# RWKV stage: the k projection first, the elementwise chain written between the weight splits of r and v

## The chip, the cores and the metric

The kernel runs on one core of a Trainium2 chip. The metric is the device time of one execution in microseconds, as the median of several runs. The core has a matrix engine (TensorE, PE in the rows), a vector engine (VectorE, DVE), an activation engine (ScalarE, ACT), GpSimd (POOL), and SyncE (SP), which here issues all the transfers. Each engine works through its own instructions in written order and waits for others on semaphores.

## The reference, cut to what matters

The whole computation is a chain of transformer stages on 256 tokens of width 1024 (`T` = 256, `D` = 1024, `C` = 8 chunks of 128 features). The change touches one of them, the RWKV7 time mixing of the second layer:

```python
xx = jnp.pad(h, ((0, 0), (1, 0), (0, 0)))[:, :-1] - h
xr, xw, xk, xv, xa, xg = [h + xx * mu[i] for i in range(6)]
r = xr @ w_r
w = -jax.nn.softplus(-(w0 + jnp.tanh(xw @ w1) @ w2)) - 0.5
k = xk @ w_k
v = xv @ w_v
a = jax.nn.sigmoid(a0 + (xa @ a1) @ a2)
g = jax.nn.sigmoid(xg @ g1) @ g2
kk = heads(k * k_k)
kk = kk / jnp.maximum(jnp.sqrt(jnp.sum(kk * kk, -1, keepdims=True)), 1e-12)
k = k * (1 + (a - 1) * k_a)
decay = jnp.exp(-jnp.exp(heads(w)))
def step(state, inp):
    sa = jnp.einsum('bhij,bhj->bhi', state, -kk_t)
    state = (state * d_t[:, :, None, :] + sa[..., None] * (kk_t * a_t)[:, :, None, :]
             + v_t[..., None] * k_t[:, :, None, :])
    return state, jnp.einsum('bhij,bhj->bhi', state, r_t)
bonus = jnp.sum(r_ * k_ * r_k.astype(f32), -1, keepdims=True) * v_
```

`exp(-exp(w))` is `exp(-KAPPA * sigmoid(...))` with `KAPPA` = exp(-0.5), so that running sums of the sigmoid (`gs`) give the decays. The recurrence is done in chunks of 64 tokens. For that, the chain computes `A = -kk * (decay up to the token before)`, `B = kk * a * growth`, `K = k * growth` and `R = r * decay`, where `decay` is exp(-KAPPA gs) and `growth` is exp(KAPPA gs).

A second task is woven in: `mod = cs @ ada_w[i] + ada_b[i]` for two later layers ("modulation"), with 48 weight slots of 1 MB.

## The kernel before, in words

Weights come through a ring of six slots of 1 MB (`Weights`, `RING`); SyncE issues the loads in one order written out in advance, each after the signals that free its slot. A product in fp32 is made of three products of split operands (`mm3`, lines 714 to 716): every slot holds two *units* of 128 output columns, ScalarE writes the high part of a unit's weights (`split_act`, line 672), VectorE the remainder (`split_dve`, line 678), and TensorE then does 24 products (`columns_pe`). The sources are split likewise (lines 696 and 704). `depth` is the number of buffers for split units, 2 in this stage.

The stage runs as follows. The norm; the shifted difference `xx`; six mixings `h + xx * mu` (line 1976), of which two buffers `m0` and `m1` hold two at a time; four low-rank hidden products (line 2002) and sixteen output products (line 2011) that give `sg` and `a`; then 24 units in the order r, k, v. Behind unit 23 stands the elementwise chain: scans, the sum of squares per head by TensorE (`heads_pe`, line 1989), Ln and Exp for its inverse root, then kk, A, the k factor, k, the bonus sums, K and R on VectorE and ScalarE, and `sum_before`, `b` and `B` on GpSimd (lines 2189 to 2194).

Between the steps of this chain `Modulation.fill` puts pieces: a piece is the column sum of the one before (line 1882), eight products with a weight slot (line 1893) and a copy by ScalarE (line 1901). 5, 5 and 2 pieces are written into the chain; the others come one per step of the inverses in the blocks (11 steps) and two ahead of each of a block's two chunks.

Four *blocks* (`block_pe` and its companions) do the recurrence, one for 512 features and 128 tokens each; a block begins with twelve transposes (line 2232). Behind them are the normalisation, the gate and the output product.

Of the kernel before, what the change touches and what calls it, by code (L numbers as in the profile page):

```python
# [110 lines left out]
def lay_out(a):  # L111
# [19 lines left out]
    for layer in range(2):  # L131
# [32 lines left out]
        else:  # L164
            for n in range(6):
                pk.features(f"mu{n}", a["c_mu"][0, n])
            by_columns(np.concatenate([a["c_w1"][0], a["c_a1"][0]], 1))
# [4 lines left out]
            for n in ("r", "k", "v"):  # L172
                by_columns(a[f"c_w_{n}"][0])
# [1741 lines left out]
class Rwkv(Stage):  # L1915
# [5 lines left out]
    def setup(self):  # L1921
# [16 lines left out]
        for _ in range(3):  # L1938
            self.plan_units(4, column_half)
# [5 lines left out]
        self.bufs = [{m: isb(f"{m}{par}", [P, 4, P]) for m in ("nt", "rb", "rk", "t", "tt", "x", "nl")} for par in range(2)]  # L1945
        self.lv, self.S = isb("LakV", [P, 4, P]), [isb(f"state{i}", [P, 4, P]) for i in range(2)]
# [15 lines left out]
    MIXES = ((1, 0), (4, 1), (5, 0), (0, 1), (2, 0), (3, 1))  # L1962

    def mix_free(self, x):
        n = self.n
        return (None, None, ("lora_hidden", n, 0), ("lora_hidden", n, 1), ("lora_hidden", n, 3), ("source_lo", n, 0, C - 1))[x]

    def mix_dve(self, e, x):
        k, n = self.k, self.n
        mu, b = self.MIXES[x]  # L1970
        if x == 0:
            e.wait_ge(*k.ge("x_shifted", n, 1))
        if self.mix_free(x) is not None:
            e.wait_ge(*k.ge(*self.mix_free(x)))
        for c in range(C):
            e.scalar_tensor_tensor(out=(self.m0, self.m1)[b][:, c, :], in0=self.xx[:, c, :], scalar=k.par(f"mu{mu}")[:, c:c + 1], in1=k.h[:, c, :],
                                   op0=ALU.mult, op1=ALU.add).then_inc(*k.up("mixed", n, x, c))


    HIDDEN = ((0, 0, 0, 64, ACT.Tanh), (1, 0, 64, 64, ACT.Copy), (2, 1, 0, 128, ACT.Sigmoid), (2, 1, 128, 32, ACT.Sigmoid))  # L1980
# [9 lines left out]

    def pe(self, e):
        k, n = self.k, self.n
        self.begin(e)
        self.norm_pe(e)
        for h, (x, s, lo, m, fn) in enumerate(self.HIDDEN):
# [16 lines left out]
        self.x_r = self.x_r_in  # L2012
# [27 lines left out]

    def act(self, e):
        k, n = self.k, self.n
        al = lambda x: x[:, :, :]
        e.activation(k.cs[:, :], k.par("c"), ACT.Silu).then_inc(*k.up("silu_c"))
        self.norm_act(e)
# [8 lines left out]
        for g, dst in enumerate((self.r, self.kk_, self.v)):  # L2054
            self.source_act(e, g, (self.m0, self.m1)[self.MIXES[3 + g][1]], [("mixed", n, 3 + g, c) for c in range(C)], ("unit", n, 8 * g - 1) if g else None)
            if g == 0:
                self.split_act(e, 0)
# [1417 lines left out]
```

## Time and profile before

| what | value |
|---|---|
| median of 3 runs | 3248.66 us (3248.07 to 3249.14) |
| the profiled execution, its own time | 3248.56 us |
| its span | 3246.8 us |
| PE busy | 2895.2 us (89%) |
| DVE busy | 1331.3 us (41%) |
| ACT busy | 1123.0 us (35%) |
| POOL busy | 243.4 us (7%) |
| DMA | 695.33 MB, 214 GB/s on average |

Times in the rows are counted from the span's start. TensorE is the busiest engine over the whole span, but the share is a mean over many stages; the RWKV stage lies between about 915 and 1500 us. A matmul in fp32 appears in the trace as two instructions, so a count there is twice the written one. `PEclk` is the clock that TensorE was granted, as a share of 2.4 GHz.

### The profile page before, as it was taken

The page shows a single profiled execution, that of the slowest core. Times are in us where ns is not written, and L with a number is a line of the kernel's source. Part 1 is how long each engine was busy: PE and PEld are TensorE (multiplying, and loading weights), DVE is VectorE, ACT ScalarE, POOL GpSimd, SP SyncE. Part 2 cuts the span into 40 slices and gives each one's busy share as a digit, 9 for nine tenths or more (in the row PEclk, how much of TensorE's full clock was granted, in tenths as well). Part 3 has the DMA queues.
Part 4 walks back from the last instruction along what each step waited for, and adds up shares of the span by engine and source line. Part 5 has one row for each costly group of instructions (what it writes and reads, how often), then busy time and mean ns, then how long its engine had stood idle before and what let it go on. Part 6 is the DMA issues. An engine that isn't in the chain of part 4 may idle for free.

```text
span 3246.8 us, 44500 instructions
## 1 busy us (share of the span) xinstructions
PE 2895.2 (89%) x18572; PEld 2276.4 (70%) x18572; DVE 1331.3 (41%) x2102; ACT 1123.0 (35%) x1974; POOL 243.4 (7%) x189
## 2 busy tenths in 40 slices
PE   8989668989978698878989899999987878999997
PEld 6879557878858477857878666666676866666665
DVE  5555465555445533435545322122185552122122
ACT  5443335454344222125443222222255242222222
POOL 1000001010000222311001000000010510000000
PEclk9999579999989799979999999999988889999999
DMA  7523105535424455115424399999832024999995
GB/s 326 193 80 143 40 26 207 189 117 213 167 79 177 148 194 185 50 40 202 187 100 164 152 398 415 415 416 415 364 118 91 1 77 172 410 419 416 415 417 229
DMA packets 95542, 695.33 MB, mean 214 GB/s; under 512 B 10592, under 2 KB 10720, under 8 KB 11232
## 3 DMA queue, kind: packets, MB, share of 16 engines
q1 hardware_dynamic: 95328, 692.32, 54.2%
q8 instruction: 153, 2.51, 0.3%
q14 instruction: 61, 0.50, 0.0%
HBM read 691.23 MB, written 1.05 MB: 213 GB/s over the span
## 4 chain that ended last, share of the span: by engine, by line
PE 84%; DVE 8%; ACT 5%; issue 2%; POOL 1%; DMA 0%; ACTq 0%; SPq 0%; DVEq 0%; POOLq 0%
PE bank L1459 14%; PE bank L714 12%; PE bank L716 11%; PE bank L715 11%; PE bank L1519 7%; PE bank L1437 4%; PE bank L1546 4%; PE bank L1781 2%; PE bank L1789 2%; PE bank L1793 1%; PE bank L2241 1%; PE bank L1893 1%; PE bank L1343 1%; PE bank L1328 1%; PE bank L1331 1%
## 5 line engine op out<-in xcount | busy, mean ns | idle before, releaser
L1459 PE MATMUL bank<-weight_ring,packed_h 128*64 128x256 f32 x2176 | 285.4, 379 | 0.0
L714 PE MATMUL bank<-source_hi_lo,weight_hi_lo 128*128 128x256 f32 x864 | 256.2, 297 | 28.1 <-DVE source_hi_lo L704 11.9
L1459 PE MATMUL bank<-more_slots,packed_h 128*64 128x256 f32 x1920 | 257.0, 379 | 1.5 <-ACT packed_h L1446 1.5
L714 PE MATMUL bank<-gate_up_hi_lo,x_hi_lo 128*128 128x512 f32 x640 | 254.0, 397 | 0.0
L716 PE MATMUL bank<-gate_up_hi_lo,x_hi_lo 128*128 128x512 f32 x640 | 249.8, 390 | 0.0
L715 PE MATMUL bank<-source_hi_lo,weight_hi_lo 128*128 128x256 f32 x864 | 249.4, 289 | 0.0
L715 PE MATMUL bank<-gate_up_hi_lo,x_hi_lo 128*128 128x512 f32 x640 | 249.2, 389 | 0.0
L716 PE MATMUL bank<-source_hi_lo,weight_hi_lo 128*128 128x256 f32 x864 | 249.0, 288 | 0.0
L1459 PEld LDWEIGHTS bank<-weight_ring,packed_h 128*64 128x64 f32 x2176 | 196.7, 137 | 73.9 <-issue 18.1
L678 DVE TENSOR_TENSOR weight_hi_lo<-weight_ring,weight_hi_lo 128x1024 fp32r<-128x1024 f32 x138 | 168.2, 1222 | 133.9 <-ACT weight_hi_lo L672 133.9
L1459 PEld LDWEIGHTS bank<-more_slots,packed_h 128*64 128x64 f32 x1920 | 174.3, 137 | 69.5 <-issue 15.4
L1475 DVE TENSOR_TENSOR packed_hidden<-packed_silu,bank 128x256 f32<-128x256 f32 x64 | 27.0, 422 | 416.5 <-ACT packed_silu L1468 416.5
L714 PEld LDWEIGHTS bank<-source_hi_lo,weight_hi_lo 128*128 128x128 f32 x864 | 169.8, 197 | 34.3 <-issue 29.9
L1536 DVE SCALAR_TENSOR_TENSOR expert_out_hi_lo<-bank,place_gates,expert_out_hi_lo 128x512 fp32r<-128x512 f32 x128 | 96.1, 751 | 223.5 <-ACT expert_out_hi_lo L1530 223.5
L672 ACT ACTIVATE weight_hi_lo<-weight_ring 128x1024 fp32r<-128x1024 f32 x144 | 150.9, 1052 | 62.8 <-PE bank L716 57.1
L838 DVE TENSOR_TENSOR down_hi_lo<-weight_ring,down_hi_lo 128x1024 fp32r<-128x1024 f32 x72 | 87.8, 1224 | 203.2 <-ACT down_hi_lo L832 203.2
L715 PEld LDWEIGHTS bank<-source_hi_lo,weight_hi_lo 128*128 128x128 f32 x864 | 170.9, 198 | 0.2
L716 PEld LDWEIGHTS bank<-source_hi_lo,weight_hi_lo 128*128 128x128 f32 x864 | 170.5, 197 | 0.0
L1468 ACT ACTIVATE packed_silu<-bank 128x256 f32<-128x256 f32 x64 | 24.6, 384 | 403.7 <-PE bank L1459 403.7
L1519 PE MATMUL bank<-weight_ring,hidden_T 128*64 128x512 f32 x544 | 146.0, 598 | 10.4 <-issue 10.4
L832 ACT ACTIVATE down_hi_lo<-weight_ring 128x1024 fp32r<-128x1024 f32 x72 | 75.8, 1058 | 221.9 <-PE bank L716 221.9
L824 DVE TENSOR_TENSOR gate_up_hi_lo<-weight_ring,gate_up_hi_lo 128x1024 fp32r<-128x1024 f32 x120 | 143.0, 1227 | 9.9 <-ACT gate_up_hi_lo L817 9.9
(524 smaller groups left out, 5645.9 us busy)
## 6 DMA issues: line engine op xcount, KB each, us to landing
weight_ring<-weight_slots SPq DMA_DIRECT2D x443, 1024.0 KB, 6.9
more_slots<-weight_slots SPq DMA_DIRECT2D x212, 1024.0 KB, 9.2
params_sb<-small_params SPq DMA_DIRECT2D x1, 3215.0 KB, 18.0
x_sb<-x_T SPq DMA_DIRECT2D x1, 1024.0 KB, 5.1
out_T<-x_sb SPq DMA_DIRECT2D x4, 256.0 KB, 2.2
params_sb<-small_params SPq DMA_DIRECT2D x1, 73.5 KB, 4.9
```

Of the source, the lines that this page charges most:

```text
L672: e.activation(self.shaped(w[:, 0, :], src), src, ACT.Copy).then_inc(*k.up("weights_hi", self.n, u))
L678: e.tensor_tensor(self.shaped(w[:, 1, :], src), src, self.shaped(w[:, 0, :], src).bitcast(F32), ALU.subtract).then_inc(*k.up(*self.lo_key(u)))
L714: e.matmul(out, w[0], x[0], start=start, stop=False, skip_group_check=shared)
L715: e.matmul(out, w[0], x[1], start=False, stop=False, skip_group_check=shared)
L716: return e.matmul(out, w[1], x[0], start=False, stop=stop, skip_group_check=shared)
L824: e.tensor_tensor(lo, src, hi.bitcast(F32), ALU.subtract).then_inc(*k.up(*self.lo_key("gate_up", j, m)))
L838: e.tensor_tensor(lo, src, hi.bitcast(F32), ALU.subtract).then_inc(*k.up(*self.lo_key("down", b, fc)))
L1437: mm = e.matmul(ps[:, j * T:(j + 1) * T], self.h_tok[:, part, q, c * P:(c + 1) * P], self.sel[g % 2][:, q, :, :].rearrange("p e s -> p (e ...
L1459: mm = e.matmul(ps[x * CAP:(x + 1) * CAP, m * FB:(m + 1) * FB], self.hc[:, c, (2 * (p % 2) + x) * CAP:(2 * (p % 2) + x + 1) * CAP], wt[:, ...
L1519: mm = e.matmul(ps[x * CAP:(x + 1) * CAP, :], self.turned[p % 2][:, fc * P + x * CAP:fc * P + (x + 1) * CAP], wd[:, fc * D + m * 512:fc * ...
L1536: e.scalar_tensor_tensor(out=self.out[p % 2][:, 1, cut], in0=k.banks.at(n, "down", p, m)[:, :], scalar=self.slot_gate[:, p % 2:p % 2 + 1], ...
L1546: mm = e.matmul(k.bank[b][:, :], self.scatter[p % 2][:, b // 2 * P:b // 2 * P + P], self.out[p % 2][:, part, b % 2 * 512:b % 2 * 512 + 512 ...
```

## The change

The k weights come first in the weight stream, ahead of the low-rank ones, and are multiplied first. All six mixings have a place of their own (in buffers that are filled later: `sg`, `a`, `y`, `r`, `v`), so they are written between the splits of the k units. The buffer depth goes from 2 to 3. The elementwise chain is written between the splits of the r and v units, some of it on another engine: scaling by `k_k` and the k factor move from VectorE to ScalarE, `B` from GpSimd to VectorE, `sum_before` and its exponential are gone, since A takes the decay of the token before by a view shifted by one inside each chunk of 64, and the two steps of r times k times `r_k` are one operation. No modulation piece stands ahead of the blocks any more. The buffer `mod_rows` lives only with the blocks.

```diff
             for n in range(6):
                 pk.features(f"mu{n}", a["c_mu"][0, n])
+            by_columns(a["c_w_k"][0])
             by_columns(np.concatenate([a["c_w1"][0], a["c_a1"][0]], 1))
...
-            for n in ("r", "k", "v"):
+            for n in ("r", "v"):
...
-        self.product_buffers(inner, depth=2)
+        self.product_buffers(inner, depth=3)
...
+    MU = (2, 1, 4, 5, 0, 3)
+    def mixed(self, x):
+        return (self.m0, self.sg, self.a, self.k.y, self.r, self.v)[x]
...
     def pe(self, e):
...
+        for u in range(8):
+            self.unit_pe(e, u)
         for h, (x, s, lo, m, fn) in enumerate(self.HIDDEN):
...
+        self.heads_pe(e, "kk", self.xx, ("kk_squared", n), "kk_sums")
...
-        for u in range(24):
-            ps = k.banks.take(e, (n, "unit", u), ("rkv", n, u))
-            self.columns_pe(e, u, ps[:, 0:T], u // 8 if u % 8 == 0 else None)
-        self.mod.fill(e, "PE", 5)
-        self.heads_pe(e, "kk", self.xx, ("kk_squared", n), "kk_sums")
-        self.mod.fill(e, "PE", 5)
-        self.heads_pe(e, "bonus", self.xx, ("rk_scaled", n, C - 1), "bonus")
-        self.mod.fill(e, "PE", 2)
+        for u in range(8, 24):
+            self.unit_pe(e, u)
+        self.heads_pe(e, "bonus", self.m0, ("rk_scaled", n, C - 1), "bonus")
...
+    def early_act(self, e):
+        self.begin(e)
+        self.split_act(e, 0)
+    def unit_act(self, e, u):
+        k, n, c = self.k, self.n, u % 8
+        if u + self.depth - 1 < 24:
+            self.split_act(e, u + self.depth - 1)
+        e.wait_ge(*k.ge("unit", n, u))
+        e.activation((self.kk_, self.r, self.v)[u // 8][:, c, :], k.banks.at(n, "unit", u)[:, 0:T], ACT.Copy).then_inc(*k.up("rkv", n, u))
...
     def act(self, e):
...
+        for u in range(8, 24):
+            if u == 16:
+                self.source_act(e, 2, self.mixed(5), [("mixed", n, 5, c) for c in range(C)], ("unit", n, 15))
+            self.unit_act(e, u)
+            if u == 8:
+                e.wait_ge(*k.ge("kk_sums", n, "kk", 3))
+                e.activation(al(inv), al(inv), ACT.Ln, scale=65536.0).then_inc(*k.up("kk_log", n))
+            elif u == 9:
+                e.wait_ge(*k.ge("kk_log", n))
+                e.activation(al(inv), al(inv), ACT.Exp, scale=-0.5).then_inc(*k.up("kk_inverse", n))
+            elif u == 10:
+                e.wait_ge(*k.ge("log_sums", n, C - 1))
+                e.activation(al(k.h), al(gs), ACT.Exp, scale=self.KAPPA).then_inc(*k.up("growth", n))
+            elif u == 11:
+                e.activation(al(k.y), al(gs), ACT.Exp, scale=-self.KAPPA).then_inc(*k.up("decay", n))
...
     def dve(self, e):
...
+        for u in range(8):
+            self.unit_dve(e, u)
+            for x in range(5 * u, 5 * u + 5):
+                self.mix_dve(e, 1 + x // C, x % C)
+        self.source_dve(e, 1, self.mixed(4))
...
+        for u in range(8, 24):
+            if u == 16:
+                self.source_dve(e, 2, self.mixed(5))
+            self.unit_dve(e, u)
+            if u == 10:
+                e.wait_ge(*k.ge("kk_inverse", n))
+                e.scalar_tensor_tensor(out=al(kk), in0=al(kk), scalar=256.0, in1=al(inv), op0=ALU.mult, op1=ALU.mult).then_inc(*k.up("kk", n))
+            elif u == 12:
+                e.wait_ge(*k.ge("kk", n))
+                e.wait_ge(*k.ge("decay", n))
+                e.scalar_tensor_tensor(out=chunks(sg)[:, :, 1:], in0=chunks(kk)[:, :, 1:], scalar=-1.0, in1=chunks(decay)[:, :, 0:63], op0=ALU.mult, op1=ALU.mult).then_inc(*k.up("A", n, 0))
...
     def pool(self, e):
         k, n = self.k, self.n
...
-        e.wait_ge(*k.ge("chunk_decay", n))
+        e.wait_ge(*k.ge("bonus", n, "bonus", 3))
```

**VectorE, from the last weight splits on.** Before, all the splits stand ahead of the chain (`weight_hi_lo` is a split, line 678; `mixed` is `gs` or `kk` here, `x_shifted` a scratch buffer, and the row of line 2124 is the scan):

```order
L704 TENSOR_TENSOR source_hi_lo_4<-mixed_4,source_hi_lo_4 128x256 x8
L678 TENSOR_TENSOR weight_hi_lo_4<-weight_ring,weight_hi_lo_4 128x1024 x7
L2124 SCALAR_TENSOR_TENSOR mixed_4<-params_sb,decay 128x256
L2125 TENSOR_SCALAR mixed_4<-k,params_sb 128x256
```

After, from the splits for units 10, 11 and 12 to the source of v (`a` is multiplied by growth in `h_sb` and by kk in `mixed`):

```order
L678 TENSOR_TENSOR weight_hi_lo_4<-weight_ring,weight_hi_lo_4 128x1024 x3
L2161 SCALAR_TENSOR_TENSOR mixed_4<-mixed_4,x_shifted 128x2048
L678 TENSOR_TENSOR weight_hi_lo_4<-weight_ring,weight_hi_lo_4 128x1024 x2
L2165 SCALAR_TENSOR_TENSOR decay<-mixed_4,y_sb 128x32x63
L2166 TENSOR_SCALAR decay<-mixed_4 128x32
L678 TENSOR_TENSOR weight_hi_lo_4<-weight_ring,weight_hi_lo_4 128x1024
L2169 TENSOR_TENSOR a<-a,h_sb 128x2048
L678 TENSOR_TENSOR weight_hi_lo_4<-weight_ring,weight_hi_lo_4 128x1024
L2172 TENSOR_TENSOR a<-a,mixed_4 128x2048
L678 TENSOR_TENSOR weight_hi_lo_4<-weight_ring,weight_hi_lo_4 128x1024
L2174 TENSOR_TENSOR k<-k,mixed_4 128x2048
L704 TENSOR_TENSOR source_hi_lo_4<-v,source_hi_lo_4 128x256 x8
```

The five long operations of the chain now stand between splits for units 10 to 17, and the last three ahead of the source of v.

**TensorE, from the end of the projections to the first inverse.** Before (line 1989 is a head sum, 1882 and 1893 a modulation piece, 2232 the transposes of the first block):

```order
L1893 MATMUL bank<-weight_ring,silu_c 32x256 x8
L1989 MATMUL bank<-x_shifted,params_sb 128x512 x4
L1882 MATMUL bank<-params_sb,mod_rows 128x1 x2
L1893 MATMUL bank<-weight_ring,silu_c 32x256 x8
L1882 MATMUL bank<-params_sb,mod_rows 128x1 x2
L1893 MATMUL bank<-weight_ring,silu_c 32x256 x8
L2232 MATMUL bank<-params_sb,a 128x128 x4
```

After, with the head sums in line 1987 and the transposes in line 2262:

```order
L716 MATMUL bank<-source_hi_lo_4,weight_hi_lo_4 128x256
L1987 MATMUL bank<-mixed_4,params_sb 128x512 x4
L2262 MATMUL bank<-params_sb,a 128x128 x4
L2262 MATMUL bank<-params_sb,k 128x128 x4
L2262 MATMUL bank<-params_sb,v 128x128 x4
```

The first piece now stands behind the first block's masked products; the head sums of k are up between the hidden and the output products of the low-rank rows.

## Rows read from the trace of the kernel before

**Rows 1.** Busy time per engine in each stage; the first line names the columns.
```profile
core 0: us, PE busy (x) PEld busy (x) DVE busy (x) ACT busy (x) POOL busy (x), PEclk, DMA share, GB/s
...
959.60:1042.80 83.20, 76.50 (x580) 75.39 (x584) 39.55 (x55) 35.43 (x62) 0.00 (x0) 0.92 0.42 148
1042.80:1106.18 63.38, 35.52 (x253) 18.12 (x251) 40.10 (x50) 19.46 (x21) 16.47 (x4) 0.71 0.51 189
1106.18:1189.08 82.90, 75.93 (x741) 64.80 (x737) 27.24 (x43) 17.36 (x37) 21.21 (x20) 0.96 0.57 204
...
1272.44:1342.08 69.64, 61.71 (x562) 55.18 (x560) 28.85 (x44) 13.88 (x28) 20.30 (x18) 0.98 0.26 92
```

**Rows 2.** Chain of waits, 1042 to 1107: start us, length us, what.
```profile
1049.96 4.52 POOL y_sb L2189
...
1079.65 6.51 DVE x_shifted L2142
```

**Rows 3.** Timeline: start, length, engine, line, operation, count [idle before <-releaser].
```profile
915.45 3.10 ACT L530 ACTIVATE y_sb<-x_sb 128x256 f32<-128x256 f32 x8 [1.18 <-DVE x_sb L628]
...
929.36 6.42 DVE L1976 SCALAR_TENSOR_TENSOR mixed<-x_shifted,params_sb,h_sb 128x256 f32<-128x256 f32 x16
...
947.19 7.17 PE L2011 MATMUL bank<-lora_hidden,weight_ring 64*128 64x256 f32 x32
```

**Rows 4.** The same of SyncE's DMA issues, 900 to 910.
```profile
905.94 0.33 SPq L395 DMA_DIRECT2D weight_ring<-weight_slots  x1
```

**Rows 5.** VectorE by shape: count | busy us, mean ns | idle.
```profile
L678 DVE TENSOR_TENSOR weight_hi_lo<-weight_ring,weight_hi_lo 128x1024 fp32r<-128x1024 f32 x24 | 29.3, 1225 | 40.7 <-ACT weight_hi_lo L672 40.7
L1976 DVE SCALAR_TENSOR_TENSOR mixed<-x_shifted,params_sb,h_sb 128x256 f32<-128x256 f32 x47 | 19.0, 478 | 1.0 <-PE bank L2002 1.0
L704 DVE TENSOR_TENSOR source_hi_lo<-mixed,source_hi_lo 128x256 fp32r<-128x256 f32 x24 | 8.3, 417 | 11.9 <-ACT source_hi_lo L696 11.9
L2142 DVE TENSOR_TENSOR x_shifted<-r,k 128x2048 f32<-128x2048 f32 x1 | 6.5, 6499 | 0.0
...
L2140 DVE TENSOR_TENSOR k<-k,x_shifted 128x2048 f32<-128x2048 f32 x1 | 2.3, 2292 | 0.0
```

**Rows 6.** Timeline of ScalarE: two copies of k units, six apart.
```profile
996.80 0.39 ACT L2063 ACTIVATE k<-bank 128x256 f32<-128x256 f32 x1 [1.71 <-PE bank L716]
...
1014.43 0.38 ACT L2063 ACTIVATE k<-bank 128x256 f32<-128x256 f32 x1 [1.68 <-PE bank L716]
```

**Rows 7.** TensorE by shape, 930 to 1110.
```profile
L2002 PE MATMUL bank<-mixed,weight_ring 128*128 128x256 f32 x16 | 3.7, 386 | 0.0
```

**Rows 8.** Timeline of TensorE in the blocks and just behind them.
```profile
1146.86 0.51 PE L1882 MATMUL bank<-params_sb,mod_rows 128*128 128x1 f32 x4
...
1311.83 0.51 PE L1882 MATMUL bank<-params_sb,mod_rows 128*128 128x1 f32 x4
...
1357.07 0.63 PE L1769 MATMUL bank<-params_sb,tt 128*128 128x128 f32 x4 [0.78 <-DVE tt L1818]
1359.35 1.09 PE L1769 MATMUL bank<-params_sb,tt 128*128 128x128 f32 x4 [1.65 <-DVE tt L1818]
...
1410.79 3.67 PE L1989 MATMUL bank<-y_sb,params_sb 128*128 128x512 f32 x8 [0.80 <-ACT y_sb L2328]
```

**Rows 9.** Timeline of ScalarE around one table load.
```profile
1066.65 1.28 ACT L2073 ACT_TABLE_LOAD   x1
1067.95 1.91 ACT L2073 ACTIVATE x_shifted<-x_shifted 128x2048 f32<-128x2048 f32 x1
```

**Rows 10.** Busy time per engine, the first v unit.
```profile
1017.66:1022.29 4.63, 4.63 (x26) 4.63 (x27) 3.34 (x8) 0.91 (x1) 0.00 (x0) 0.63 0.22 28
```

**Rows 11.** Timeline of TensorE, modulation pieces at the slow clock.
```profile
1073.62 1.01 PE L1882 MATMUL bank<-params_sb,mod_rows 128*128 128x1 f32 x4 [0.56 <-ACT mod_rows L1901]
...
1077.06 1.02 PE L1882 MATMUL bank<-params_sb,mod_rows 128*128 128x1 f32 x4 [0.56 <-ACT mod_rows L1901]
```

**Rows 12.** DMA issues of the profile page: count, KB each, us to landing.
```profile
weight_ring<-weight_slots SPq DMA_DIRECT2D x443, 1024.0 KB, 6.9
```

More of the change, by code:

```diff
@@ L1937, in setup @@
         w.done(s[2], ("lora_out", self.n, 1, C - 1))
-        for _ in range(3):
+        for _ in range(2):
             self.plan_units(4, column_half)
@@ L1959, in setup, with mix_dve @@
         self.plan_units(3, row_half)
[L1962 to L1980, printed above, removed]
+    MU = (2, 1, 4, 5, 0, 3)
+    def mixed(self, x):
+        return (self.m0, self.sg, self.a, self.k.y, self.r, self.v)[x]
+    def mix_dve(self, e, x, c):
+        k = self.k
+        e.scalar_tensor_tensor(out=self.mixed(x)[:, c, :], in0=self.xx[:, c, :], scalar=k.par(f"mu{self.MU[x]}")[:, c:c + 1], in1=k.h[:, c, :],
+                               op0=ALU.mult, op1=ALU.add).then_inc(*k.up("mixed", self.n, x, c))
+    SOURCES = (0, 4, 5)
+    HIDDEN = ((1, 0, 0, 64, ACT.Tanh), (2, 0, 64, 64, ACT.Copy), (3, 1, 0, 128, ACT.Sigmoid), (3, 1, 128, 32, ACT.Sigmoid))
     def heads_pe(self, e, tag, src, signal, empty, lhs="half_ones"):
@@ L2043, in act @@
         al = lambda x: x[:, :, :]
+        kk, inv, gs = self.m1, self.xx, self.sg
         e.activation(k.cs[:, :], k.par("c"), ACT.Silu).then_inc(*k.up("silu_c"))
         self.norm_act(e)
+        self.x_r = self.x_r_in
+        for u in range(1, self.depth - 1):
+            self.split_act(e, u)
+        self.source_act(e, 0, self.mixed(0), [("mixed", n, 0, c) for c in range(C)])
+        for u in range(8):
+            self.unit_act(e, u)
+            e.wait_ge(*k.ge("rkv", n, u))
+            e.activation(kk[:, u, :], self.kk_[:, u, :], ACT.Copy, scale=k.par("k_k")[:, u:u + 1]).then_inc(*k.up("kk_scaled", n, u))
+        e.wait_ge(*k.ge("mixed", n, 5, C - 1))
+        e.wait_ge(*k.ge("kk_scaled", n, C - 1))
+        e.activation(al(inv), al(kk), ACT.Square).then_inc(*k.up("kk_squared", n))
         for h, (x, s, lo, m, fn) in enumerate(self.HIDDEN):
+            if h == 2:
+                self.source_act(e, 1, self.mixed(4), [("mixed", n, 4, c) for c in range(C)], ("unit", n, 7))
             e.wait_ge(*k.ge("lora_hidden", n, h))
@@ L2052, in act @@
                 e.activation(dst[:, c, :], k.banks.at(n, "lora", h, c)[:, 0:T], ACT.Sigmoid, bias=k.par(bias)[:, c:c + 1]).then_inc(*k.up("lora_sigmoid", n, h, c))
-        self.x_r = self.x_r_in
[L2054 to L2057, printed above, removed]
-            for c in range(C):
-                u = 8 * g + c
-                if u + 1 < 24:
-                    self.split_act(e, u + 1)
-                e.wait_ge(*k.ge("unit", n, u))
-                e.activation(dst[:, c, :], k.banks.at(n, "unit", u)[:, 0:T], ACT.Copy).then_inc(*k.up("rkv", n, u))
@@ new lines, in dve @@
+        for c in range(C + 2):
+            if c < C:
+                self.mix_dve(e, 0, c)
+            if c >= 2:
+                self.source_lo(e, 0, self.mixed(0), c - 2)
+        for u in range(1, self.depth - 1):
+            self.split_dve(e, u)
+        e.tensor_scalar(self.one_less[:, :], k.par("k_a"), -1.0, 1.0, ALU.mult, ALU.add).then_inc(*k.up("one_less", n))
+        for u in range(8):
+            self.unit_dve(e, u)
+            for x in range(5 * u, 5 * u + 5):
+                self.mix_dve(e, 1 + x // C, x % C)
@@ L2303, in block_act @@
         if it == 0:
[L2304 removed]
+            e.wait_ge(*k.ge("bonus", n, "bonus", 3))
         for name in "BKV":
```

126 lines of the change are left out of this document (53 added, 73 removed).

## The prediction

> **What bounds the kernel now.** I read the busy share by stage first, then the chain of waits, then the single instructions of the stretch. The reader is to see in the stages [rows 1] that the projections (959.60 to 1042.80) are 92% TensorE, that the recurrence blocks are about 90% TensorE as well, but that between them lie 63.38 us (1042.80 to 1106.18) in which no engine is busy for more than 40.10 us and the clock averages 0.71. In the chain [rows 2] this gap is one dependency path that hops from engine to engine: among its steps a GpSimd subtraction of 4.52 us and an r times k product of 6.51 us on VectorE. TensorE fills part of it with twelve of the 48 modulation pieces, and still idles.
>
> **What the change does with this path.** The k projection comes first, so that everything that needs only k and the low-rank rows can run on VectorE and ScalarE while TensorE does r and v. After v only the bonus sums are left. The price is in three places: the engines that split weights (ScalarE high part, VectorE low part) get elementwise work in their queues ahead of the splits; two stretches wait for mixed sources; the twelve pieces move into the recurrence blocks.
>
> **Step 1, k.** Up to 929.36 nothing moves but one split: its 1.05 us on ScalarE go where ScalarE waited 1.18 us for VectorE's sums [rows 3], its low half on VectorE beside TensorE's sum of squares, so I cost it at nothing; without that cover it would be 2.3. The weights for it are in: the last of the ring's six slots was asked for at 905.94, k's first long before [rows 4]. From 929.36 VectorE does 8 mixings at 19.0/47 = 0.404 and 8 source remainders at 8.3/24 = 0.346, together 6.0, then a split of 1.22 [rows 5]; unit 0 runs beside it. Unit 1 starts at 936.7. A unit of 24 products takes (1014.43 - 996.80)/6 = 2.94 [rows 6]; in the same time VectorE must do a split and five mixings, 1.22 + 2.02 = 3.24. There is some lead from depth 3, so I take 7 units at 2.9: k ends at 957.0. VectorE's last mixing ends at 936.7 + 8 x 3.24 = 962.6.
>
> **Step 2, low-rank rows.** Four hidden products at about 3.6 (3.7 for the one of full width [rows 7]), the k head sums at 3.5 (the same sums of y, warm, took 3.67 with the last one's drain [rows 8]), the output products 7.2 [rows 3]: 14.4 + 3.5 + 7.2 = 25.1, to 982.1. The square waits for the last mixing and is ready at 964.6, the sums start at 971.4: hidden. The r source, the sums' clamp and the scans lie beside these products (8 scans of 0.6 end near 981).
>
> **Step 3, r.** This is the stretch on which the sum depends. ScalarE's queue, from 982.6: split 10, copy 8, table load and Ln (3.2); split 11, copy 9, table load and Exp (3.2); split, copy, Exp (1.9), twice; split, copy, four factors (1.3), twice. A split is 1.05, a copy 0.3. That is 6 x 1.35 + 6.4 + 3.8 + 2.6 = 20.9 us for six units, in which TensorE could do seven. The lead is two units. Followed in order: high halves ready 983.6, 989.5, 994.1, 997.3, 1000.6, 1003.2; VectorE adds 1.22 to each, and its 2.29 us operations (kk after split 12, A after split 14) push low halves 13 and 15 to 998.9 and 1005.5. TensorE waits 0.2, 1.7, 0.6, 0.1 and 0.7 before units 11, 12, 13, 14 and 15, and ends r at 1008.4: 8 units, 23.2, plus 3.1 of waits, 26.3. Then the v source: VectorE has from 1005.5 the products a x growth, B and k x factor (3 x 2.29) and two splits between them (2 x 1.22), to 1014.8, and only then the first remainder. TensorE waits from 1008.4 to 1015.2, 6.8 us. So of this stretch 9.9 us are waits.
>
> A table load stands now twice in the queue that feeds TensorE. In the trace the load starts at 1066.65 right after Ln, takes 1.28, and Exp starts at 1067.95, 0.02 behind it [rows 9]; I use that. The Trainium skill, page "ScalarE: Activation LUTs", section "What ACT_TABLE_LOAD costs", gives a drain of about 1.38 us for every switch on top of the load. By that rule ScalarE would be 2.8 us later, and the time up to 2.8 longer, about 3201; the trace speaks for no such drain where the load follows an activation at once.
>
> **Step 4, v and the bonus.** The first v unit comes after idle time: the one of before needed 4.63 us at a clock of 0.63, after a wait of 6.2 [rows 10]. I take 4.8 for the same and 7 x 2.94 = 20.6, to 1040.6. VectorE has in this time 6 splits, 8 fused r x k products, K, R and a copy: 7.3 + 3.2 + 4.6 + 0.2 = 15.3 of 25, so that TensorE sets the pace. The bonus sums are 3.5: the blocks begin at 1044.1. Before they began at 1106.18. **Term one: 1044.1 - 1106.2 = -62.1.**
>
> **Step 5, GpSimd.** It loses its three operations here. The r times k product took 6.50 us while GpSimd was multiplying, where the same form takes 2.29 alone [rows 5]; both gone, which is in the times above.
>
> **Step 6, the first block.** Its transposes ran slow (2.6 us from 1106.18 to the first masked product; warm 12 x 0.11 = 1.3) and the first products too. Now TensorE comes in busy, but VectorE needs two row products (0.9) behind the last bonus. **Term two: -1.8**, bounds 0 and -2.5.
>
> **Step 7, the moved pieces.** Each block calls for up to 15 pieces (11 inverse steps, two pairs of two). Before, 12 were done ahead and blocks 0 and 1 took 30, block 2 the last six and a closing column at 1311.83. Now blocks 0, 1 and 2 take 45 and block 3 three and the column. Block 2 will be as block 0 was from the same point: from 1146.86 to its end at 1189.08 is 42.2, before it was 1311.83 to 1342.08, 30.3 [rows 1, 8]: +12.0. In block 3 the first two pieces stand where TensorE waited 0.78 and 1.65 for VectorE [rows 8], so they cost nothing, the third 1.3 and the column 0.4. **Term three: +13.7**; bounds 0 (all in waits) and 12 x 3.44 = 41, the pitch of pieces at the slow clock (1077.06 - 1073.62) [rows 11]. I take the warm value because block 0 did 15 of them at a clock of 0.96 [rows 1]. The modulation weights are asked for as v's slots come free, six of them before the blocks, and the blocks of before had only 57% DMA at most.
>
> **Sum.** 3248.56 (the profiled execution) - 62.1 - 1.8 + 13.7 = 3198.4. The median of the runs is 3248.66, the same to 0.1. Operations that the trace does not show: the factor on ScalarE (0.32 by source copies, 0.44 by the sigmoids, at most 1 us in all), A on a strided view (2.29 flat; twice that would add 2.3 to VectorE's queue). Its own range is 3188.5 (all 9.9 us of waits in r and v covered) to 3208 (0.6 us more for each of the 16 units).
>
> **The rivals.**
> A, the queues bind harder: ScalarE and VectorE work in turn, with no overlap between them, through r and v. In r that is 8 x (1.05 + 0.3) + 12.8 on ScalarE and 8 x 1.22 + 5 x 2.29 on VectorE, 44.8 us; in v 8 x 0.35 + 6 x 1.05 + 8 x 0.3 and 8 x 0.35 + 15.3, 29.6; with the bonus 77.9 against the 62.0 taken from 982.1 to 1044.1: +16, 3214. For it: both engines work in written order, and a split waits behind every long operation. Against it: before, in the projections, both engines were busy for under half of the time [rows 1], and depth 3 lets a split run two units ahead.
> B, the slow clock: short waits in r, and moved pieces at 1.2 GHz. The trace shows after the wait before v a clock of 0.63 for the next 4.6 us [rows 10]. If it stayed low through the r units, eight would take 5.1 (24 products of 256 columns at 1.2 GHz) instead of 2.9, +18, and with half of the pieces at 3.44 instead of 1.44, +12: 3228. Against it: the waits in r are 0.1 to 1.7 us. The Trainium skill, page "TensorE: Matmul & The Clock Gate", section "A second HAM failure mode: psum-queue depth-cycling", tells of a kernel whose frequent short idles made the clock swing; blocks 0 and 2, with short waits between their products, stay at 0.96 and 0.98 here [rows 1] and speak against it.
> C, slower than before: the modulation weights become the bound. All 48 slots of 1 MB are now read from the first block on. If a piece had to wait for its own transfer, 6.9 us each by the profile page's median from issue to landing [rows 12], they would take 331 us instead of the 259 forecast for 48 pieces: +72, 3270. It decides from 259/48 = 5.4 us per slot on and makes the kernel slower from 6.5. Against it: block 0 moved 204 GB/s, that is 5.1 us a slot, with six in flight and no wait on them.
> D, no change: A and B together and half of C's waits between, or a chain that stays behind v because one early operation is late. It needs some 50 us in a stretch of 115.
>
> **How the numbers follow.** My forecast 0.75, A 0.12, B 0.08, C 0.03, D 0.02. The range goes from 3188 to 3226: it takes in the likeliest case's own range, A and most of what lies between A and B. What this kernel's measurement can tell from no change is 0.2%, 6.5 us; all of the forecast, A and B are faster by more: faster 0.95, same 0.02, slower 0.03.
>
> **What would show it.** Blocks beginning near 1044 show steps 1 to 4; k ending at 957 and r starting at 982 the first two; one wait of about 7 us before the first v unit and a handful under 2 us in r the third; if instead every r unit waits, A. A block 2 of some 82 us and a block 3 of some 79 show step 7; a block 0 longer than before, B or C. A ScalarE gap of over 1 us behind a table load would give the drain its place. The forecast is wrong if the first block begins after 1054, or if the four blocks together grow by more than 20.

## The result, and the profile after

The changed kernel takes 3200.17 us (median of 4 runs, 3198.04 to 3207.63) against 3248.65 (3248.07 to 3249.14): ratio 0.9853, interval [0.9841, 0.9865]. Its profiled execution is the longest of the four, 3207.63 us; two later sets of runs of the same kernel gave 3197.8 (3194.43 to 3199.89) and 3199.81 (3199.62 to 3202.65).

I cut both traces at the same events: VectorE's last row of the shifted difference, 0.2 us ahead of the first mixing (932.17 here, 929.16 before), the first transposes of each block, and the first head sum behind the blocks. The busy time per engine in these stretches of the changed kernel, the part up to the blocks cut finer:

```profile
core 0: us, PE busy (x) PEld busy (x) DVE busy (x) ACT busy (x) POOL busy (x), PEclk, DMA share, GB/s
932.17:959.98 27.81, 25.81 (x193) 25.47 (x194) 27.77 (x59) 17.17 (x30) 0.00 (x0) 0.88 0.42 146
959.98:984.91 24.93, 24.93 (x104) 16.21 (x104) 14.78 (x30) 15.58 (x32) 0.00 (x0) 1.00 0.27 92
984.91:1011.20 26.29, 24.19 (x193) 23.29 (x192) 14.27 (x11) 24.22 (x32) 0.00 (x0) 1.00 0.52 189
1011.20:1018.03 6.83, 0.00 (x0) 0.03 (x1) 6.83 (x6) 3.65 (x10) 0.00 (x0) 0.71 0.31 106
1018.03:1045.81 27.78, 27.78 (x201) 25.82 (x202) 18.93 (x27) 7.81 (x13) 0.00 (x0) 0.95 0.39 137
1045.81:1127.82 82.01, 73.91 (x734) 62.46 (x732) 28.12 (x41) 16.76 (x36) 21.83 (x20) 0.98 0.54 193
1127.82:1211.18 83.36, 74.53 (x738) 63.03 (x736) 28.39 (x45) 17.33 (x37) 20.33 (x18) 0.98 0.52 190
1211.18:1294.12 82.94, 75.47 (x739) 64.12 (x737) 27.31 (x39) 17.33 (x37) 20.33 (x18) 0.96 0.52 191
1294.12:1365.09 70.97, 60.14 (x502) 55.00 (x501) 30.56 (x45) 13.47 (x27) 20.31 (x18) 0.93 0.13 45
```

To the blocks it is 113.64 us where it was 177.02; the stretch of 63.38 us between projections and blocks [rows 1] is gone. Of the five new stretches only the fourth, 6.83 us, has no TensorE work. The blocks took 82.90, 83.36, 69.64 and 68.71 us; now they take 82.01, 83.36, 82.94 and 70.97. The stage is 48.7 us shorter. (The profiled execution shows 40.9 less: it is 3.0 us late before the stage and loses another 4.8 behind it, in code that is the same in both kernels. The two later profiles of it don't have this, see K.)

What the chain of waits goes through in r and ahead of v (start, length, what ended):

```profile
988.50 1.28 ACT L2085
...
1003.39 1.62 ACT mixed L2099 x4
...
1008.58 2.29 DVE a L2169
...
1012.01 2.20 DVE a L2172
...
1015.35 2.20 DVE k L2174
1017.55 0.35 DVE source_hi_lo L704
```

From 988 on it is ScalarE's queue, from 1008.58 the three products on VectorE, and then the source of v. TensorE itself waited for two things there:

```profile
PE bank L714 <- DVE source_hi_lo L704: 7.0, 1, 7.0
PE bank L714 <- DVE weight_hi_lo L678: 1.8, 3, 1.3
```

### The profile page after: what moved, and what is told of

Read it like the earlier page. It is cut to its first block, busy times and chain, and to the rows that moved or that the text cites. A ratio compares the mean times of both kernels' runs of the same rounds, so it can differ in the third digit from the quotient of the medians.

```text
span 3205.8 us, 44502 instructions
## 1 busy us (share of the span) xinstructions
PE 2885.6 (90%) x18572; PEld 2274.2 (71%) x18572; DVE 1321.1 (41%) x2088; ACT 1127.3 (35%) x1988; POOL 227.5 (7%) x186
## 4 chain that ended last, share of the span: by engine, by line
PE 85%; DVE 7%; ACT 5%; issue 2%; POOL 0%; DMA 0%; ACTq 0%; SPq 0%; DVEq 0%
PE bank L1459 14%; PE bank L714 12%; PE bank L716 11%; PE bank L715 11%; PE bank L1519 7%; PE bank L1437 4%; PE bank L1546 4%; PE bank L1781 2%; PE bank L1789 2%; PE bank L1793 1%; PE bank L1893 1%; PE bank L2271 1%; PE bank L543 1%; PE bank L1343 1%; PE bank L1328 1%
## 5 line engine op out<-in xcount | busy, mean ns | idle before, releaser
L714 PEld LDWEIGHTS bank<-source_hi_lo,weight_hi_lo 128*128 128x128 f32 x864 | 169.1, 196 | 40.9 <-issue 37.5
L672 ACT ACTIVATE weight_hi_lo<-weight_ring 128x1024 fp32r<-128x1024 f32 x144 | 150.9, 1051 | 63.4 <-PE bank L716 57.7
```

The source lines that it names most:

```text
L672: e.activation(self.shaped(w[:, 0, :], src), src, ACT.Copy).then_inc(*k.up("weights_hi", self.n, u))
L714: e.matmul(out, w[0], x[0], start=start, stop=False, skip_group_check=shared)
```

## The experiments

All of them are compared with the kernel before on the same chip. A to E were timed in 3 rounds, F to L in 5. Unless said otherwise an edit is on the changed kernel.

### A. The whole chain behind the last v unit (e1)

```diff
         for u in range(8, 24):
             self.unit_act(e, u)
+        for u in range(8, 24):
             if u == 8:
...
         for u in range(8, 24):
             self.unit_dve(e, u)
+        for u in range(8, 24):
             if u == 10:
```

> The changed kernel, but every operation of the elementwise chain that stood between the splits of r and v now stands behind the last v unit, in the same order. Theory (the chain itself became short, and only part of the gain is that it is hidden): no waits in r, v ends 100 us after the first mixing, then Ln and Exp 6.4, growth and decay 3.8, factor 2.6, a x growth, B and k x factor 6.9, r x k 3.2, bonus sums 5.5 on a slow clock; the blocks begin some 129 us after the first mixing instead of 113.4, and the time is about 3217. Rival (hiding is the whole gain, the chain costs its old 63 us once it stands alone): about 3250.

Measured: 3216.3 us (3214.63 to 3218.11), ratio 0.9897 [0.988, 0.9913]. The stretch to the blocks took 131.95 us, and TensorE's waits in it were:

```profile
PE bank L1987 <- DVE mixed L2182: 24.7, 1, 24.7
PE bank L714 <- DVE source_hi_lo L704: 1.3, 1, 1.3
```

So k first and the shorter chain, with the chain still behind v, already give 45.1 of the 63.4 us to the blocks. Of these, 12.5 lie ahead of the end of v (v ends 101.1 us after the start of the stretch, the projections of before 113.6), and 32.5 behind it (30.9 us instead of 63.4). The stretch behind v has also lost its twelve pieces; no run here separates what that gives from what the shorter chain gives. Writing the chain between the splits gives the other 18.3, and 16 in the medians. The interleaving is the smaller part of the change.

### B. The last twelve pieces cut short (e2)

```diff
-            for fc in range(2):
+            for fc in range(2 if q < 36 else 1):
...
-        for c in range(C):
+        for c in range(C) if p < 36 else (0,):
```

> The changed kernel with the last 12 of the 48 modulation pieces cut short: one product with the weight slot instead of eight, one column sum instead of two (this part of the modulation is left out, the weights are still loaded). These are as many pieces as moved into the blocks. Theory (TensorE sets the pace there, so pieces cost their own time): 1.44 goes to about 0.3 each; block 2 shorter by about 10, the time about 3189. Rival (they fill waits): no change, 3199 to 3201.

Measured: 3198.78 us (3196.88 to 3200.08), ratio 0.9844 [0.9827, 0.986]. By the time alone the rival holds. The windows of its blocks 2 and 3 say something else:

```profile
1208.06:1282.30 74.24, 66.83 (x597) 57.02 (x595) 27.30 (x39) 17.33 (x37) 20.32 (x18) 1.00 0.58 213
1282.30:1354.64 72.34, 60.89 (x452) 56.22 (x451) 30.32 (x45) 13.47 (x27) 20.35 (x18) 0.88 0.13 44
```

Block 2, where nine of the cut pieces are, took 74.24 us at a clock of 1.00. The same block of the uncut kernel took 80.15 at 1.00 (rows under H), so cutting a piece saves 0.66 us there: pieces do cost time, though less than the 1.14 us that I expected. But block 3, with three pieces cut, took 72.34 us at a clock of 0.88, where the uncut kernel took 70.97 at 0.93 and, in its two later profiles, 70.01 at 0.95. Why the clock was lower here isn't shown. The time of this run can't be read without the clock, which opened the question that F to J take up.

### C. Buffer depth 2 again (e3)

```diff
-        self.product_buffers(inner, depth=3)
+        self.product_buffers(inner, depth=2)
```

> The changed kernel with 2 buffers for split units instead of 3. Theory (the third buffer is what lets long operations stand between the splits): in r a unit waits for 0.4 + the long operation + 1.05 + 1.22 - 2.9, so 3.0, 3.0, 1.7, 1.7 and about 1.5 twice, some 12 us of waits in r instead of 3; k about 1.6 longer; the time about 3212. Rival (the lead does not matter, the engines have slack): 3200 to 3202.

Measured: 3204.43 us (3200.12 to 3204.85), ratio 0.9856 [0.9839, 0.9872]; not to be told from the changed kernel. To the blocks it took 117.73 us, 4.1 more than the first profile of the changed kernel (3.2 more than the two later ones): k 0.8, r 1.0, and 2.1 in the first v unit, which ran at a lower clock (first this run, then the changed kernel):

```profile
1015.21:1021.73 6.52, 6.52 (x32) 6.52 (x33) 2.20 (x7) 0.96 (x1) 0.00 (x0) 0.54 0.22 94
```

```profile
1018.03:1022.41 4.38, 4.38 (x26) 4.38 (x27) 3.34 (x8) 0.00 (x0) 0.00 (x0) 0.68 0.34 142
```

My 12 us were wrong. TensorE waited for split weights five times in r, 3.6 us in all, against three times and 1.8 us at depth 3. Behind r stands the wait for the source of v, still 7.0 us, and ScalarE's queue sets the pace of r at either depth.

### D. The source of v ahead of the products that can wait (e4)

```diff
-            elif u == 14:
-                e.wait_ge(*k.ge("a_grown", n))
-                e.tensor_tensor(al(a), al(a), al(kk), ALU.mult).then_inc(*k.up("B", n))
-            elif u == 15:
+            elif u == 16:
                 e.tensor_tensor(al(kx), al(kx), al(factor), ALU.mult).then_inc(*k.up("k_scaled", n))
...
                 e.tensor_copy(self.pend[:, :, :], decay[:, :, 63:T:64]).then_inc(*k.up("chunk_decay", n))
+                e.wait_ge(*k.ge("a_grown", n))
+                e.tensor_tensor(al(a), al(a), al(kk), ALU.mult).then_inc(*k.up("B", n))
```

> The changed kernel with B moved behind the last split of v and k x factor behind the source of v, on VectorE. Theory: TensorE's wait of 6.7 us before v falls to about 1, the clock stays up and the first v unit takes 2.9 instead of 4.8; VectorE has 10 us to spare in v. The blocks begin 7 to 8 us earlier, the time about 3192. Rival: the two operations come back as waits in v or ahead of the bonus, 3198 to 3201.

Measured: 3193.35 us (3189.97 to 3197.12), ratio 0.9824 [0.9808, 0.9841]. VectorE (timeline) now comes to the source right behind two splits, and B goes to the end:

```profile
1001.51 2.29 DVE L2169 TENSOR_TENSOR a<-a,h_sb 128x2048 f32<-128x2048 f32 x1 [0.78 <-ACT mixed L2099]
...
1005.99 2.76 DVE L704 TENSOR_TENSOR source_hi_lo<-v,source_hi_lo 128x256 fp32r<-128x256 f32 x8
...
1026.24 2.28 DVE L2186 TENSOR_TENSOR a<-a,mixed 128x2048 f32<-128x2048 f32 x1
```

```profile
PE bank L714 <- DVE source_hi_lo L704: 2.6, 1, 2.6
```

The wait fell from 7.0 to 2.6 us, not to nothing: ScalarE rounds the source only from 1004.30 on, after its last copy of r, and takes 2.55. Nor did the clock stay up: the first v unit took 4.3 us, not 2.9, and the second 3.25 at a clock of 0.89. The first:

```profile
1006.56:1010.83 4.27, 4.27 (x26) 4.27 (x27) 4.27 (x9) 1.24 (x3) 0.00 (x0) 0.68 0.66 246
```

To the blocks it is 109.93 us, 3.7 less than in the first profile and 4.6 less than in the two later ones, where I had expected 7 to 8. The edit helps for the reason given, by about half of what I gave it. That the time of the kernel came out near my 3192 all the same is in part luck: in this profile block 0 had the full clock and took 80.38 us, against 82.01 to 83.60 in the changed kernel's three.

### E. The kernel before, its two products on VectorE instead of GpSimd (e5)

```diff
+        e.tensor_tensor(al(a), al(kk), al(a), ALU.mult).then_inc(*k.up("b", n))
...
+        e.wait_ge(*k.ge("b", n))
+        e.tensor_tensor(al(a), al(a), al(t4), ALU.mult).then_inc(*k.up("B", n))
```

(the same lines are taken out of GpSimd's program; `b` is the product of kk and a.)

> The kernel before with one part of the change alone: the two products that GpSimd computed (b and B) are computed by VectorE, one after the other, and nothing else is moved. Theory (the two engines slow each other down): kk takes 2.3 us instead of 6.50 and A about 2.7 instead of 6.3, b adds 2.3 to VectorE and B lies in a VectorE idle time of 1.98; the blocks start about 5 us earlier and the kernel takes about 3243.5. Rival (kk and A are slow by themselves and GpSimd only saved work): they keep 6.5 and 6.3 us, VectorE gains 2.6 to 4.6 us of work on the path, and the kernel takes 3251 to 3253.

Measured: 3242.21 us (3238.47 to 3245.05, 10 runs), ratio 0.9978 [0.9969, 0.9987]. The timeline of VectorE:

```profile
1080.95 2.29 DVE L2141 TENSOR_TENSOR a<-mixed,a 128x2048 f32<-128x2048 f32 x1
1083.15 2.29 DVE L2143 TENSOR_TENSOR x_shifted<-r,k 128x2048 f32<-128x2048 f32 x1
1085.47 2.19 DVE L2146 TENSOR_SCALAR x_shifted<-x_shifted,params_sb 128x256 f32<-128x256 f32 x8
...
1096.20 2.29 DVE L2153 TENSOR_TENSOR a<-a,y_sb 128x2048 f32<-128x2048 f32 x1
```

My expectation calls the two slow operations kk and A. That was a slip: they are the product of r and k (6.51 us [rows 2]), which ran beside GpSimd's b, and the eight scalings by `r_k` behind it, which ran beside GpSimd's B. They take 2.29 and 2.19 us here, with b and B (1080.95, 1096.20) as two more operations on VectorE, and the path to the blocks is 5.4 us shorter (171.61 against 177.02). So the two engines held each other up. The Trainium skill has it so for the first of the two, page "SBUF — State Buffer", section "Who interferes with whom": a VectorE instruction with two inputs in SBUF contends with a GpSimd instruction that reads SBUF. The runs agree: 6.51 us against 2.29. In the kernel before, VectorE and GpSimd did this:

```profile
1079.65 6.50 DVE L2142 TENSOR_TENSOR x_shifted<-r,k 128x2048 f32<-128x2048 f32 x1
1086.19 6.30 DVE L2145 TENSOR_SCALAR x_shifted<-x_shifted,params_sb 128x256 f32<-128x256 f32 x8
```

```profile
1077.37 6.63 POOL L2191 TENSOR_TENSOR a<-mixed,a 128x2048 f32<-128x2048 f32 x1 [22.90 <-DVE x_shifted L2138]
1085.83 4.67 POOL L2194 TENSOR_TENSOR a<-a,y_sb 128x2048 f32<-128x2048 f32 x1 [1.82 <-ACT y_sb L2076]
```

The cost looks like a wait and not like a slower rate. GpSimd's b ends at 1084.00 and r times k 2.15 us later, about the 2.29 that it takes alone; B ends at 1090.50 and the scalings 1.99 us later, against 2.19 alone.

### F and G. Pieces in the blocks' waits (e6, e7)

On D, with `n` = 1 in e6 and 2 in e7:

```diff
         for par in range(2):
             bf = self.bufs[par]
+            if par:
+                self.mod.fill(e, "PE", n)
```

(and the matching calls of ScalarE and VectorE.) Here, between the masked products of a block's two halves, TensorE waits 2.8 to 3.0 us for VectorE.

> The version with the v source first (3193.4 us in its own runs) and one modulation piece of each block moved to where TensorE waits 2.8 to 3.0 us for the masks of a new block. Theory (a piece costs its own 0.9 to 1.0 us only where TensorE has other work): pieces in these four waits cost nothing, so the kernel is 2 to 4 us faster than that version, 3189 to 3191.5. Rival (a piece pushes what stands behind it wherever it is written, or the gain comes back as a slower clock): no change within 1 us, 3193 to 3195.

> As the kernel above, with two pieces in each of the four waits. Theory: two pieces take 1.9 to 2.0 us and still fit in a wait of 2.8 to 3.0 us less the 0.2 to 0.6 us that the masked products' eviction needs behind them, so this costs at most 0.6 us per block and saves the own time of four more pieces: 3188.5 to 3191, within 1 us of the version with one piece. Rival (pieces push wherever they stand): 3193 to 3197.

Measured: e6 3191.88 us (3187.05 to 3194.02), ratio 0.9824 [0.981, 0.9837]; e7 3188.22 us (3184.37 to 3195.71), 0.9812 [0.9799, 0.9825]. One piece is not to be told from D by time, nor two from one. Blocks 0 and 1 of e7, in windows:

```profile
1042.56:1123.22 80.66, 75.20 (x774) 62.63 (x772) 28.15 (x41) 17.53 (x38) 21.83 (x20) 1.00 0.61 223
1123.22:1205.45 82.23, 75.83 (x778) 63.21 (x777) 28.40 (x45) 18.10 (x39) 20.34 (x18) 1.00 0.61 218
```

They take 80.66 and 82.23 us at a clock of 1.00, with 20 matmuls more per piece than in the changed kernel. In e6 they took 80.40 and 81.76, also at 1.00. D's block 0, which had the clock by itself, took 80.38 with no piece in the wait. So one piece there costs 0.02 us and a second 0.3 to 0.5. And all six blocks 0 to 2 of e6 and e7 had the full clock, while of 24 such blocks in the eight kernels without it four had. In blocks 1 and 2 that made e6 1.6 and 2.8 us shorter than D, which had 0.98 and 0.96 there. It was the larger effect in these blocks, and not what I had argued for.

### H, I and J. Work that is thrown away in the same waits (a1, e8, e9)

The changed kernel, no piece moved, with the next piece's eight products done once (e8) or twice (e9) more, for nothing:

```diff
             for dst, L, Rh, mask, sign in self.MASKED:
                 ps = k.banks.take(e, (n, dst, it, par), ("masked", n, it, par, dst))
+                if dst == "nt" and par:
+                    self.mod.again_pe(e, 1)
...
+        for _ in range(times):
+            for c in range(C):
+                e.matmul(k.bank[1 + p % 2][32 * (c % 4):32 * (c % 4) + 32, 0:FB], ...)
```

> The changed kernel beside the two below on one chip, to compare them with; 3197.8 to 3200.2 us by its medians so far. Its profile shows which of the first three blocks held the clock: by the runs so far 4 of 24 such blocks had a mean clock of 1.00 where TensorE waits 3 us behind the first masked products, and 6 of 6 where that wait was filled with pieces.

> The changed kernel with more work and none moved: in each block's wait between the masked products of the two halves, TensorE also does the eight products of the next modulation piece once, and throws them away. Theory (the 3 us wait is what makes the clock fall a few us later, and filling it alone keeps the clock): blocks 0 to 2 show a mean clock of 1.00 and take about 80.4, 81.8 and 80.2 us, 3 to 6 us less in sum than the 248.3 and 246.9 us of the changed kernel's two profiles, and the kernel takes about 3194 to 3196 us although it does more. Rival (the clock of the blocks is chance, and the pieces in the two versions before won by being moved): clocks of 0.96 to 1.00 as before, 3198 to 3201 us.

> The same with the eight products done twice, about 1.9 us of the 3 us wait. Theory: clocks of 1.00 in blocks 0 to 2 again, 3194 to 3196 us, and no more than with one set, since nothing is left to gain there. Rival: clocks as before and 3198 to 3202 us.

Measured: a1 3199.81 us (3199.62 to 3202.65), ratio 0.9851 [0.9836, 0.9867]; e8 3198.25 (3196.18 to 3200.48), 0.9843 [0.983, 0.9857]; e9 3192.39 (3189.71 to 3194.33), 0.9824 [0.9811, 0.9838]. The four blocks of a1 and of e9:

```profile
1044.74:1128.33 83.59, 75.48 (x733) 63.35 (x731) 28.13 (x41) 16.78 (x36) 21.84 (x20) 0.96 0.52 190
1128.33:1211.46 83.13, 74.31 (x738) 62.80 (x736) 28.38 (x45) 17.35 (x37) 20.32 (x18) 0.98 0.51 190
1211.46:1291.61 80.15, 72.68 (x738) 61.34 (x737) 27.30 (x39) 17.35 (x37) 20.32 (x18) 1.00 0.54 198
1291.61:1361.62 70.01, 59.19 (x503) 54.15 (x501) 30.55 (x45) 13.49 (x27) 20.32 (x18) 0.95 0.13 46
```

```profile
1045.49:1125.83 80.34, 74.17 (x765) 61.77 (x764) 28.15 (x41) 16.78 (x36) 21.84 (x20) 1.00 0.54 197
1125.83:1207.54 81.71, 74.81 (x771) 62.35 (x769) 28.40 (x45) 17.35 (x37) 20.37 (x18) 1.00 0.53 194
1207.54:1287.64 80.10, 74.56 (x770) 62.26 (x768) 27.33 (x39) 17.35 (x37) 20.34 (x18) 1.00 0.55 198
1287.64:1355.95 68.31, 59.42 (x534) 53.53 (x533) 30.58 (x45) 13.48 (x27) 20.35 (x18) 0.98 0.13 47
```

e9 does more on TensorE (765 instructions in block 0 against 733) and is 3.25, 1.42, 0.05 and 1.70 us shorter in the four blocks, exactly in those where the clock had not been 1.00. All runs of e9 are below all of a1. e8 shows the same blocks 0 to 2 (80.34, 81.68, 80.10 at 1.00), but 70.88 at 0.93 in block 3, and its time fell by only 1.6 us, less than the theory's 4 to 6 and not outside the spread. Its stage took 427.56 us, 3.9 less than a1's 431.42; its profile lost the same 3.9 us again behind the stage (see K). So the theory on the clock is borne out by the blocks of both versions, and its time only by e9, which came out below the range that I gave. What the wait does, in the timeline of a1, block 0:

```profile
1049.73 1.06 PE L2271 MATMUL bank<-r,x 128*128 128x128 f32 x8
1053.59 1.19 PE L2271 MATMUL bank<-decay,t 128*128 128x128 f32 x8 [2.80 <-DVE x L2370]
1054.57 1.92 PE L2271 MATMUL bank<-decay,x 128*128 128x128 f32 x8
...
1057.97 1.06 PE L2271 MATMUL bank<-r,x 128*128 128x128 f32 x8
```

Eight masked products take 1.06 us before the wait of 2.80 us. A microsecond behind it the same eight take 1.92, and at 1057.97 again 1.06: the clock went to 1.2 GHz for about 3.4 us. Each such dip costs half its length. Block 0 of a1 has a second one, behind a wait of 1.48 us that ends at 1063.88; the window of it shows a clock of 0.60:

```profile
1064.00:1068.00 4.00, 4.00 (x30) 2.71 (x30) 0.00 (x0) 0.98 (x2) 1.09 (x1) 0.60 0.63 221
```

In e8 and e9, with the longer wait filled, both are gone.

### K. The changed kernel again (a0)

> The changed kernel again, beside the kernels below on one chip. Its median so far is 3200.2 us with single runs from 3198.0 to 3207.6. If the 3 us that its profiled run had lost before the stage and the 6.6 us after it belong to no edit, its median is again 3198 to 3202 (ratio 0.984 to 0.986). If they came with the kernel, each run carries them and the median is 3204 or more.

Measured: 3197.8 us (3194.43 to 3199.89), ratio 0.9843 [0.983, 0.9856]. Its stage took 431.4 us (114.56 to the blocks; 83.60, 83.12, 80.15, 70.01), a1's 431.4 too, the first profile's 432.9. The 3.0 and 4.8 us lost outside the stage are not the change's. The 4.8 are no accident of one run either: from the first head sum behind the blocks to the end of the span, eight of the fourteen profiles (before, a0, a1, e1, e5, e6, e9, e10) take 1835.8 to 1836.7 us and the other six (the first of the changed kernel, e2, e3, e4, e7, e8) 1840.2 to 1840.7, in the same code. The clock differs between 200 and 400 us behind the blocks, here in a1 and then in e8:

```profile
1561.62:1761.62 200.00, 176.03 (x1026) 153.98 (x1025) 103.17 (x152) 88.06 (x146) 16.26 (x11) 0.94 0.40 147
1557.45:1757.45 200.00, 176.25 (x1007) 154.95 (x1006) 103.18 (x152) 85.70 (x145) 16.26 (x11) 0.91 0.40 143
```

So single times of the changed kernel and its versions can carry some 4 us that no edit put there (and the stretch begins at 924.7 us in one profile and at 932.7 in another), and the stage, read from the trace, tells more of an edit than the median does.

### L. All together (e10)

G, and sixteen products for nothing in the wait of block 3.

> The v source first, two modulation pieces in each block's wait, and in the fourth block, where none are left, sixteen products for nothing in that wait. If the three gains add up: 109 to 110 us to the blocks (114.5 in the changed kernel), blocks of 80.7, 82.2 and 77.6 us at a clock of 1.00, and a fourth block of 66 to 68.5 at 0.95 or more: 415 to 418 us for the stage instead of 431 to 433, and a kernel of 3184 to 3188 us. If the clock falls elsewhere instead (the fourth block has the least work, and stood at 0.88 with two pieces in the waits), its block takes 70 us or more and the kernel 3188 to 3192.

Measured: 3186.21 us (3185.44 to 3186.44), ratio 0.9806 [0.9792, 0.9819], the fastest version here. Its stage took 417.73 us: 109.90 to the blocks, then 80.64, 82.23, 77.64 and 67.32, the first three at 1.00 and the last at 0.92. The gains add up as expected, but for the fourth block's clock, for which I had said 0.95 or more.

## Why the prediction was right

The forecast was 3198.4 us, the median 3200.17; the forecast for the stage was -50.2 us, measured -48.7, and -50.2 in both later profiles. The mechanism is the forecast one: the chain runs beside r and v, TensorE's one long wait stands ahead of v, and the pieces cost time in block 2. That the sum agrees to 0.1 us twice is luck, since the terms are off by up to 2.5 us in both directions. By its steps:

- Step 1, k: 27.6 us from the first mixing forecast, 27.6 measured (27.8 in the windows, which start 0.2 us ahead of it). Step 2, low-rank rows: 25.1 and 24.9.
- Step 3, r: 26.3 and 26.3, but made up otherwise: waits of 1.8 us in three (3.1 in five forecast; the five that I listed add up to 3.3), and units slightly longer, 24.2 us for the eight and not 23.2. That the totals agree is luck. The wait for the source of v was 6.8 forecast, 7.0 in the trace (6.83 in the windows). A group of four k factors on ScalarE took 2.07 us, not 1.3, and VectorE's a x growth waited 0.79 us for it. The trace of before had no activation with two column operands and I took the nearest rows. The Trainium skill, page "ScalarE: Activation LUTs", section "What ACT_TABLE_LOAD costs", prices each such operand at about 93 ns; from its figures a pitch of 0.49 us is estimated, and the trace has that (four in 2.07 us, one taking 0.60).
- The table drain: the same section would put up to 1.4 us more on each of the two table loads. The timeline of ScalarE shows no gap:

```profile
988.09 0.39 ACT L2051 ACTIVATE r<-bank 128x256 f32<-128x256 f32 x1 [1.65 <-PE bank L716]
988.50 1.28 ACT L2085 ACT_TABLE_LOAD   x1
989.79 1.92 ACT L2085 ACTIVATE x_shifted<-x_shifted 128x2048 f32<-128x2048 f32 x1
```

The load starts 0.02 us behind the copy's end and the activation 0.01 behind the load's; the measurement decides, here for no drain.
- Step 4: the first v unit took 4.38 us at a clock of 0.68 (4.8 forecast), v and the bonus 27.8 in all (28.9 forecast). Term one: -62.1 forecast, -63.4 measured; 0.4 us of the difference is the first unit, 0.4 the other seven at 2.88 instead of 2.94. In both later profiles it is -62.5.
- Step 5: shown by E. Moving GpSimd's two products alone is worth 5.4 us.
- Step 6: -1.8 forecast, -0.9 in the first profile. The masked products of the second half start like this, before and after:

```profile
1115.92 1.18 PE L2241 MATMUL bank<-decay,t 128*128 128x128 f32 x8 [2.79 <-DVE x L2340]
```

```profile
1054.66 1.76 PE L2271 MATMUL bank<-decay,t 128*128 128x128 f32 x8 [2.80 <-DVE x L2370]
```

That is 9.74 us into block 0 before and 8.85 after: the faster start is worth 0.9 us, half of the forecast, and a1 has it too (8.85). What the block gains or loses beyond that is its clock. In D and L, with the clock at 1.00, block 0 is 2.5 and 2.3 us shorter than before; at 0.96 (a1) it is 0.7 longer.
- Step 7: +13.7 forecast, +15.6 measured (block 2 +13.3, block 3 +2.3); +11.8 in a1, where block 2 had the full clock. The place of the pieces was right. That they lie where TensorE has its own work, and cost time there, is what B shows (0.66 us for each cut piece); F shows the other side, a piece in a wait that costs 0.02 us.

The rivals: A (queues bind harder) did not come, TensorE waited in three places of r and none of v, and with the chain taken out of the queues altogether (experiment A) the kernel was 16 us slower, not faster. B (slow clock) came in small: dips of 3.4 or 6.8 us in all in each of blocks 0 to 2 that has them, at a cost of 1.4 to 3.3 us a block, and none in the r units. I had dismissed the Trainium skill's section "A second HAM failure mode: psum-queue depth-cycling" (page "TensorE: Matmul & The Clock Gate") because blocks 0 and 2 stood at 0.96 and 0.98. That was the wrong reading: those figures were already a clock that swings, before the change. The section tells of frequent short idles while PSUM banks are cycled; here it is one wait of 2.8 to 3.0 us in each block, and filling it in e9 made blocks 0 to 2 4.7 us shorter than a1's and the stage 6.4. C: no wait on a transfer appears, and the DMA share of block 2 is 0.52.

## What to carry to other kernels

When a dependent chain stands behind a projection, look first for another order of the projections that lets it start early, and shorten it; writing it between the other engine's feeding work comes second (18 of 63 us here). Put the operand that the next stretch waits for ahead of everything that is not yet needed. A wait of some 3 us on TensorE costs more than itself if the clock falls behind it, so put movable work there first, and compare block times only at equal clocks.

## What the runs showed of the hardware

- A stretch of 2.8 to 3.0 us of idle TensorE in otherwise dense work is followed, in 22 of 27 blocks 0 to 2, by 3.4 or 6.8 us at 1.2 GHz in all. Filling 1.07 us of it (e8) or more with products, even useless ones, kept the clock in 15 of 15 blocks 0 to 2 (e6 to e10). Why five of the 27 unfilled ones were spared as well, I can't say from these runs.
- The fourth block, which has the least work, got 0.88 to 0.98 however it was filled. With its three pieces and nothing else added (the changed kernel, a0, a1, e1, e3, e4) it got 0.93 to 0.98, with them cut short or gone (before, e2, e5, e6, e7) 0.88 to 0.93. That less work lowers the clock is not shown by this, since each is one profile.
- The single runs of one kernel differ along with the clock they were granted: the five of e7 were 3184.37, 3187.09, 3188.22, 3190.83 and 3195.71 us at mean clocks of 0.949, 0.946, 0.948, 0.945 and 0.942.
- A VectorE product of two operands of 128x2048 takes 2.29 us alone and 6.51 beside a GpSimd product [rows 2, 5], and eight 128x256 scalings with one such operand took 6.30 instead of 2.19. The strided A, 2016 of 2048 columns in pieces of 63, takes 2.25, no more than a flat one.
